# A hybrid-mixer trunk: the first norm's scales loaded with the tokens, and the tail of the last norm reordered

## The reference

```python
def rmsnorm(x, g):
    xf = x.astype(F32)
    y = xf * lax.rsqrt(jnp.mean(xf * xf, -1, keepdims=True) + EPS)
    return (y * g.astype(F32)).astype(x.dtype)

def reference(...):
    for layer in range(DEPTH):
        h = rmsnorm(x, norm1_g[layer])
        proj = h @ w_in[layer]
...
        x = x + merged.astype(x.dtype) @ w_out[layer]
        h2 = rmsnorm(x, norm2_g[layer])
...
        x = x + f
    return rmsnorm(x, final_g)
```

## Time and profile before

| | us |
|---|---|
| median of 3 runs (1833.03 to 1833.71) | 1833.34 |
| the profiled execution | 1832.43 |
| its span | 1830.6 |
| TensorE busy in the span | 1816.6 (99%) |
| VectorE busy | 1501.2 (82%) |
| ScalarE busy | 1196.5 (65%) |
| GpSimd busy | 208.1 (11%) |
| chain that ended last, TensorE's share | 94% |

### The profile page before, as it was taken

How to read it: one execution, slowest core, us unless ns; L and a number is a source line. 1 busy time by engine, 2 the same in 40 slices (tenths; PEclk the granted TensorE clock), 3 DMA queues, 4 the chain that set the end, 5 groups by cost and what they waited for, 6 DMA issues and landing times.

```text
span 1830.6 us, 26159 instructions
## 1 busy us (share of the span) xinstructions
PE 1816.6 (99%) x9689; PEld 1552.5 (85%) x9689; DVE 1501.2 (82%) x1347; ACT 1196.5 (65%) x1030; POOL 208.1 (11%) x147
## 2 busy tenths in 40 slices
PE   9999999999999999999999999999999999999997
PEld 8998888999999988879888888888888888888886
DVE  7786687866688866787999988988898888998887
ACT  6655555544456555656678777777777777877765
POOL 1056000000020470000930000000000000000010
PEclk9999999999999999999999999999999999999999
DMA  9454445555555445454999999999999999999994
GB/s 365 172 184 163 170 174 184 184 183 183 189 199 175 170 161 184 161 187 192 379 388 379 385 376 382 375 376 389 380 380 376 379 379 382 376 384 374 387 410 171
DMA packets 74542, 521.22 MB, mean 285 GB/s; under 512 B 8176, under 2 KB 8432, under 8 KB 13680
## 3 DMA queue, kind: packets, MB, share of 16 engines
q1 hardware_dynamic: 71568, 509.34, 73.3%
q0 software_dynamic: 2912, 11.01, 1.6%
HBM read 509.83 MB, written 10.49 MB: 284 GB/s over the span
## 4 chain that ended last, share of the span: by engine, by line
PE 94%; DVE 3%; issue 1%; DMA 1%; ACT 1%; DVEq 0%; SPq 0%; ACTq 0%
PE psum L1483 92%; PE psum L1949 1%; DVE weight_raw_r L821 1%; DMA first_raw<-moe_w 1%; DVE proj_r L821 0%; PE psum L1878 0%; DMA x<-x_in 0%; DVE yb_pair L787 0%; DVE h_pair L821 0%; PE psum L1587 0%; PE psum L1712 0%; DVE proj L1209 0%; DVE y_lo L780 0%; DVE proj L1215 0%; ACT proj L749 0%
## 5 line engine op out<-in xcount | busy, mean ns | idle before, releaser
L777 DVE TENSOR_TENSOR weight_lo<-weight_raw,weight_hi 128x2048 fp32r<-128x2048 f32 x139 | 325.0, 2338 | 117.7 <-ACT weight_hi L429 116.3
L429 ACT ACTIVATE weight_hi<-weight_raw 128x2048 fp32r<-128x2048 f32 x139 | 265.4, 1911 | 102.2 <-PE psum L1483 98.2
L1483 PE MATMUL psum<-weight_hi,y_hi 128*128 128x512 f32 x768 | 305.9, 398 | 1.9 <-DVE y_lo L780 1.2
L1483 PE MATMUL psum<-weight_hi,y_lo 128*128 128x512 f32 x768 | 300.0, 391 | 0.0
L1483 PE MATMUL psum<-weight_lo,y_hi 128*128 128x512 f32 x768 | 298.9, 389 | 0.0
L1483 PE MATMUL psum<-weight_lo,y_lo 128*128 128x512 f32 x672 | 261.6, 389 | 0.0
L1483 PE MATMUL psum<-h_pair,weight_hi 128*128 128x256 f32 (+1 forms) x1152 | 228.0, 309 | 0.0
L1483 PE MATMUL psum<-weight_raw_r,y_hi 128*128 128x512 f32 x576 | 224.6, 390 | 0.0
L1483 PE MATMUL psum<-proj_r,y_hi 128*128 128x512 f32 x576 | 224.3, 389 | 0.0
L1483 PEld LDWEIGHTS psum<-h_pair,weight_hi 128*128 128x128 f32 x1152 | 186.1, 191 | 10.5 <-issue 1.8
L821 DVE TENSOR_TENSOR proj_r<-proj,weight_hi 128x2048 fp32r<-128x2048 f32 x72 | 164.7, 2288 | 28.3 <-ACT weight_hi L461 28.2
(11 more groups left out here) (308 smaller groups left out, 3156.3 us busy)
## 6 DMA issues: line engine op xcount, KB each, us to landing
proj<-moe_w SPq DMA_DIRECT2D x144, 1024.0 KB, 6.2
weight_raw<-moe_w SPq DMA_DIRECT2D x144, 1024.0 KB, 6.0
weight_raw<-mix_w SPq DMA_DIRECT2D x106, 1024.0 KB, 4.8
first_raw<-moe_w SPq DMA_DIRECT2D x48, 1024.0 KB, 6.3
weight_raw<-ff_w SPq DMA_DIRECT2D x33, 1024.0 KB, 4.7
made_rows<-zeros POOLq DMA_DIRECT2D x1, 4096.0 KB, 22.0
made_rows<-pool_tmp SPq DMA_DIRECT2D x8, 512.0 KB, 4.6
weight_raw<-mix_w SPq DMA_DIRECT2D x4, 512.0 KB, 7.9
```

The source lines that it names most:

```text
L429: A(hi[:, slot, :], raw[:, slot, :], ACT.Copy).then_inc(hi_done, 1)
L777: V.tensor_tensor(lo[:, slot, :], raw[:, slot, :], hi[:, slot, :].bitcast(f32), ALU.subtract).then_inc(lo_done, 1)
L1483: return nc.tensor.matmul(o, a, b_, start=start, stop=stop, skip_group_check=True, **k)
```

## The change

At the start, the eight columns of the first layer's norm scales are put in front of each partition's row of x, in device memory and in SBUF (`x_all`, x is a view of it behind the scales). The first half's transfer brings scales and four channel blocks in rows of 1032 floats; it is now SP's first issue. The parameters are issued behind the constants; ScalarE and VectorE wait for them only behind the first unit halves. TensorE multiplies with zeros 7 times instead of 8.

At the end, all adds of VectorE stand ahead of the products with the final scales. Only columns 0 to 511 get such a product; columns 512 on get one fused pass with the reciprocal root and the scales. ScalarE brings the root's table in before the first add, and scales columns 0 to 511 of both token blocks. The result is stored in four transfers of 256 KB, three from SP and one from ScalarE's queue.

```diff
@@ -90,6 +90,7 @@
+X_AT = (0, KT + KT // 2 * SEQ, KT + KT * SEQ)
@@ -118,7 +119,9 @@
-        x = sb("x", [P, KT, SEQ])
+        x_all = sb("x_all", [P, KT + KT * SEQ])
+        first_norm = x_all[:, 0:KT]
+        x = x_all[:, KT:].rearrange("p (k n) -> p k n", n=SEQ)
@@ -331,14 +334,14 @@
-            sp.dma_start(par[:, :PAR_FIRST], par_in[0, :, :PAR_FIRST]).then_inc(par_loaded, 16)
             for u in range(2):
                 for part in range(2):
                     if u == 0:
-                        sp.dma_start(x[:, 4 * part:4 * part + 4, :], x_in[:, 4 * part:4 * part + 4, :]).then_inc(x_loaded[part], 16)
+                        sp.dma_start(x_all[:, X_AT[part]:X_AT[part + 1]], x_in[:, X_AT[part]:X_AT[part + 1]]).then_inc(x_loaded[part], 16)
...
             sp.dma_start(con[:], con_in).then_inc(con_loaded, 16)
+            sp.dma_start(par[:, :PAR_FIRST], par_in[0, :, :PAR_FIRST]).then_inc(par_loaded, 16)
@@ -411,10 +414,12 @@
+            sp.wait_ge(S["tok_std"], 2 * TT + 1)
+            sp.dma_start(out[:, 0, 0:512], x_gain[:, 0, 0:512]).then_inc(stored, 16)
             for t in range(TT):
-                sp.wait_ge(*((S["tok_std"], 2 * TT + 1), (S["rstd_done"], 3))[t])
-                sp.dma_start(out[:, t, :], x_gain[:, t, :]).then_inc(stored, 16)
-            sp.wait_ge(stored, 16 * TT)
+                sp.wait_ge(S["rstd_done"], 3 + t)
+                sp.dma_start(out[:, t, 512:], x_gain[:, t, 512:]).then_inc(stored, 16)
+            sp.wait_ge(stored, 16 * 2 * TT)
@@ -434,7 +439,7 @@
-                gain = P_("norm2" if n % 2 else "norm1")
+                gain = P_("norm2" if n % 2 else "norm1") if n else first_norm
@@ -585,7 +590,6 @@
             for layer in range(DEPTH):
-                act.wait_ge(par_loaded, 16 * (layer + 1))
@@ -598,11 +602,13 @@
                 else:
+                    act.wait_ge(par_loaded, 16 * (layer + 1))
                     for q in range(PAIRS):
...
                 if layer == 0:
                     act.wait_ge(con_loaded, 16)
+                    act.wait_ge(par_loaded, 16)
@@ -743,20 +749,21 @@
             body(last_item, True)
+            A(small[:, 1, 0, 0:1], C_("eps"), ACT.Sqrt)
...
-                if n == 0:
-                    act.wait_ge(S["end_sq"], TT)
-                    A(small[:, 1, 0, 0:1], ssq[:, 0, 0:1], ACT.Sqrt)
...
             act.wait_ge(S["rstd_done"], 2)
-            act.wait_ge(S["end_gain"], 3)
-            A(x_gain[:, 0, :], x_gain[:, 0, :], ACT.Copy, scale=rstd[:, 0, :]).then_inc(S["tok_std"], 1)
+            for t in range(TT):
+                act.wait_ge(S["end_gain"], t + 1)
+                A(x_gain[:, t, 0:512], x_gain[:, t, 0:512], ACT.Copy, scale=rstd[:, t, :]).then_inc(S["tok_std"], 1)
+            act.wait_ge(S["tok_std"], 3 * TT)
+            act.dma_start(out[:, 1, 0:512], x_gain[:, 1, 0:512]).then_inc(stored, 16)
@@ -1068,7 +1075,6 @@
             for layer in range(DEPTH):
-                dve.wait_ge(par_loaded, 16 * (layer + 1))
...
                 dve.wait_ge(con_loaded, 16)
+                dve.wait_ge(par_loaded, 16 * (layer + 1))
@@ -1324,28 +1331,28 @@
-            def gains(n):
...
+            def gains():
+
                 for t in range(TT):
...
+                    dve.wait_ge(S["end_added"], t + 1)
+                    V.tensor_tensor(x_gain[:, t, 0:512], x_tok[:, t, 0:512], gain_row[:, 0:512], ALU.mult).then_inc(S["end_gain"], 1)
...
             ends(0)
-            gains(0)
             ends(1)
...
-            gains(1)
+            gains()
...
-            dve.wait_ge(S["end_gain"], 2 * TT)
-            V.tensor_scalar(x_gain[:, 1, :], x_gain[:, 1, :], rstd[:, 1, :], None, ALU.mult).then_inc(S["rstd_done"], 1)
+            for t in range(TT):
+                dve.wait_ge(S["end_added"], TT + t + 1)
+                V.scalar_tensor_tensor(x_gain[:, t, 512:], x_tok[:, t, 512:], rstd[:, t, :], gain_row[:, 512:], ALU.mult, ALU.mult)\
+                    .then_inc(S["rstd_done"], 1)
@@ -1779,7 +1786,7 @@
-            for _ in range(8):
+            for _ in range(7):
                 mm(bank(6), zeros[:, 0:P], zeros[:], True, True)
@@ -2066,7 +2073,7 @@
-        "x_in": q["x"][0].T.reshape(KT, P, SEQ).transpose(1, 0, 2),
+        "x_in": np.concatenate([per_channel(q["norm1_g"][0]), q["x"][0].T.reshape(KT, P, SEQ).transpose(1, 0, 2).reshape(P, -1)], 1),
```

More of the change, by code:

```diff
@@ L1325, in ends @@
                     V.tensor_tensor(x_tok[:, t, half], x_tok[:, t, half], bank((2, 6)[n] + t), ALU.add).then_inc(S["end_added"], 1)
-            def gains(n):
-                half = slice(512 * n, 512 * n + 512)
+            def gains():
                 for t in range(TT):
-                    dve.wait_ge(S["end_added"], TT * n + t + 1)
-                    V.tensor_tensor(x_gain[:, t, half], x_tok[:, t, half], gain_row[:, half], ALU.mult).then_inc(S["end_gain"], 1)
+                    dve.wait_ge(S["end_added"], t + 1)
+                    V.tensor_tensor(x_gain[:, t, 0:512], x_tok[:, t, 0:512], gain_row[:, 0:512], ALU.mult).then_inc(S["end_gain"], 1)
             dve.wait_ge(row_loaded, 16)
```

## The result

The changed kernel takes **1854.01 us** (median of 4 runs, 1853.55 to 1854.41). The kernel before took 1833.53 beside it (1833.03 to 1835.77). The ratio is 1.0109, with an interval of 1.0098 to 1.0121: slower by 20 us, where no change that could be measured was forecast. The chip granted full clock in both (mean 0.999). The profiled execution took 1853.55 us, of which the span is 1851.7, so 21.1 us more than the 1830.6 of before.

The account below looks back on a forecast made before the run. TensorE, busy 800.00 of 800 us from 900 to 1700, was taken as the bound, with start and end exposed. Gains of 0.12 (start) and 1.85 (end), 1.97 off 1833.34, gave 1831.4 us, range 1830.2 to 1832.8.

Parts of the forecast that it names:

- rival C: Tiles behind x: 32 bytes' shift slows products with a moving operand there by 6.8 ns, 10.0 us, to 1841.4; chance 0.04.
- The landing: Opening load: x lands 0.36 to 0.81 us earlier, taken as 0.42, with the parameters no longer ahead.
- rival A: Start: the gain arrives whole, x and unit 4's weights 0.81 us earlier, giving 1830.7 to 1831.1; chance 0.13.
- Does the earlier start reach the end?: At unit 4: TensorE finds bank 0 occupied until 36.16 and keeps only 0.12 us; bounds 0 and 0.81.
- The clock: TensorE's start: seven warm-ups end near 9.05, idle 0.9 us, clock stays at 2.4 GHz; cost 0, otherwise 1.5 us.
- The rule on 256-byte starts: x's load: by the skill page, 3% more beats, unit 4 0.08 us later, result 1831.5; no loss was counted.
- the first square: End, ScalarE: with the root table's load moved ahead of it, it starts 0.1 us late.
- the last square: End, ScalarE: four squares in a row, the last starting at 22.40 instead of 23.76, 1.36 us earlier.
- the first store: End: waits for a scaling of 512 columns instead of 1024, issued at 24.35 against 26.24, 1.89 us earlier.
- VectorE's two fused passes: End: two passes of 512 columns replace one of 1024, taken as 0.70 us each, bounds 0.64 and 0.84.
- ScalarE's issue: End, a store from ScalarE's queue: its issue takes between 0.42 and 1.28 us; cost 0.
- Rival B: Stores at the end: 2 KB rows flow at 270 GB/s, the last byte 1.25 us later, 1832.6; chance 0.07.

Follow-up runs that it names:

- b1: The kernel before with an unused 32-byte tile ahead of the first weight ring, so all tiles move and no distance changes: 1833.79 us, ratio 1.0002.
- a2: The kernel before with an unused tile of 64 bytes ahead of x: 1854.58 us, ratio 1.0113.
- a4: The kernel before with 32 unused bytes ahead of the y tiles only; rings, x and h_pair stay: 1856.71 us, ratio 1.0124.
- c1: The changed kernel with x_all declared behind all other tiles, so the other tiles keep their distances modulo 1024 bytes: 1831.36 us, ratio 0.9991.
- f1: c1 with nine warm-up products with zeros instead of seven: 1831.54 us in one run.
- e1: The kernel before with the change's edits of the end alone, loads and x as before: 1832.46 us, ratio 0.9992.
- a3: The changed kernel with 96 unused bytes ahead of x_all, so everything behind x moves by 128 bytes against the kernel before: 1847.05 us, ratio 1.0072.
- m1: A kernel of TensorE products alone, without the model, 24 per setting, either or both operands' starts moved by 0 to 1024 bytes: 292.26 us in all.
- m2: m1 with 48 products per setting and only the moving operand shifted, -256 to 256 bytes, finer steps: 236.5 ns a product at -16 with 512 columns.

## Why the prediction was wrong, and where it was right

**The step that failed** is rival C, "Slower", with its 0.04. I saw that the scales put all tiles behind x 32 bytes further, and gave it a price only for a *moving* operand that leaves its own grid of 64 bytes. That is not what the chip shows: b1 moves everything off the grid at no cost, a2 moves by a multiple of 64 and pays in full, a4 pays with the moving operand in place. It is the distance between tiles, in a period of 256 bytes: for most of the products that of their own two operands. The forecast's sum has no term for it, and TensorE's busy time grew by 22.7 us. The size per product, 6.8 ns, happened to be near (4 to 7 measured). What made C's sum 10.0 instead of some 22 us was the set of products. I counted 1472 with a moved moving operand; 896 of them have 256 columns and became 4 ns faster, and the other 576, proj_r with y_hi, have both operands moved alike. The shift touches every product that takes one operand from a ring and one from behind x, and 5216 of those have 512 columns.

The evidence I set against it was read from the wrong rows. run_rows' products at 280 ns against h_pair's 285 seemed to show that 32 off does no harm. They can't show it. Both are of 256 columns, and none of the 512-column products that pay is among them. The partner of run_rows, of_head, is declared right behind it, so it lies as far off 64 as run_rows does, and their distance is 1024 bytes and up to 60 more for the column used. And in b1, which puts run_rows on a multiple of 64, its mean is 280 as before: its own place was not what made it differ from 285. VectorE's products with gain_row say nothing about TensorE's two operands. No group of fp32r products with 512 columns in the trace of before had its operands off each other; that should have left C's price open from both sides and its chance well above 0.04.

**Start.** The landing was mis-sized: 0.42 expected, 1.6 to 1.7 measured. I took the parameters' bytes off at 410 GB/s; the stretch from 3.0 to 4.5 us ran at 177 GB/s with them ahead, at 381 without. That is the first half of rival A. Its second half, that unit 4's weights come as much earlier, did not happen (0.16). The step under "Does the earlier start reach the end?" holds: the gain is held up at bank 0, as c1 and f1 confirm, and of 1.52 us 0.24 are kept in after at unit 4 (0.28 in c1), against the 0.12 of the sum. At the last y_lo 0.05 of c1's are left, and by the medians it could be up to 1.1, so 0.12 is neither confirmed nor refused. The waits came a little differently than said: 0.88 us at unit 4 for the evacuation (the trace says only "issue", and the rule above is the evidence), and one of 0.56 for VectorE's normed rows, ahead of the small products on proj, that I had not seen. The clock stayed at full level with seven warm-ups. They ended at 9.39 in after and at 10.05 in c1, not at 9.05, in c1 directly ahead of the products.

**The rule on 256-byte starts** in the Trainium skill, page "DMA: Bandwidth & Descriptors", section "How a descriptor splits into AXI transactions": by it, x would carry more beats and unit 4's weights would land 0.08 later, an estimate from that page. No loss can be seen here: x lands 3.9 us after its issue, and unit 4's weights 0.16 earlier. Its part in the sum is too small for these runs to refuse it.

**End.** Right, term by term: the first square 0.05 late (0.1 said), the last square 1.49 earlier (1.36), the first store 1.92 earlier (1.89), the end 1.8 earlier (1.85), and 1.7 in e1 alone. VectorE's two fused passes took 1.41 together, as two of 0.70 would. ScalarE's issue took 0.39, just under the lower bound of 0.42. Rival B, with 270 GB/s for rows of 2 KB, is refused: the quarters flow at about 380.

**Sum.** c1 holds everything but the tiles' places, and its median is 1831.36 for a forecast of 1831.4. That it is so near is luck in part: the before of its group is 1833.58 and not 1833.34, so the gain is 2.22 where 1.97 was forecast, and c1's runs scatter from 1830.58 to 1833.67.

## What to carry to other kernels

When a tile's size changes, list where every tile behind it starts, and compare the starts of each product's moving and stationary operand modulo 256 bytes; here a distance of 0 was best for 512 columns, the moving operand 64 bytes below the stationary one for 256 columns, and an unused pad sets it. If busy time rises on an engine whose instructions have not changed, compare the groups' means with shapes apart first, and look for what moved rather than for what waits. A row that shows "no harm" counts only for the shape it has.

## What was not expected of the hardware

The dependence on distance was new to me: up to 9.6 ns of 227 at 512 columns (-16 bytes), a gain of 6.4 ns of 120 at 256 columns (-64), nothing at 128 columns. Its cause stays open. Two things don't follow from the table.

The first is the pairs that moved together. Their own distance is the same in all these kernels, and from start to start (ns) they take:

| both operands moved by | 0 (before) | 32 (after) | 64 (a2) | 128 (a3) |
|---|---|---|---|---|
| proj_r with y_hi | 227.2 | 231.1 | 237.4 | 226.2 |
| h_pair with y_hi | 226.8 | 232.2 | 235.5 | 227.2 |
| m1, both starts moved | 228.2 | 227.9 | 228.2 | 226.7 |

In after that is 3.3 of the experts' 21.6 us (576 times 3.9 ns and 192 times 5.4). These products are issued in turn with products of the rings, and a neighbour's distance may enter; but in a3 the neighbours are off by 128 and these pairs pay nothing. In b1 and c1, where the rings keep their distance too, they are as before. So the distance of a product's own two operands is not the whole story, and no run separates the rest.

The second is that m1 and m2 disagree at some settings. At a distance of -16 with 512 columns m1 (stationary operand moved) has 226.7 and m2 236.5; at +64 with 256 columns m1 has 113.3 and m2 117.8; both operands moved by 16 give 230.0 with 512 columns in m1. The absolute places differ, so the table holds for the places it was taken at, and the two kernels' 32 bytes for theirs.

The other thing that was new is what the parameters, 148 KB in rows of 1184 bytes, cost at the opening of the stream: x behind them landed 5.1 us after its issue, without them 3.9. In the six kernels with the old order it was 4.6 to 5.1, in the five with the new one 3.8 to 4.1. Their bytes alone are 0.36 us at 410 GB/s; whether the rest comes from the rows' size is not shown.
